# A hybrid block and a second layer on one core: order of weight splits, token splits and norm broadcasts changed in eight places

## The reference, cut to what matters

```
h = concat(meta[16], x[512])                       # 528 tokens, 1024 wide
z = rmsnorm(h) @ w_in                              # conv a, b | c_q 256 | c_kv 128 | k_rope 32
conv = silu(layernorm(conv31(a * sigmoid(b)) + conv_b))            # depthwise, 512 channels, 31 taps
attn = causal attention, 8 heads, 64 + 32 rotated dims, q from c_q, k and v from c_kv
h += concat(rmsnorm(attn), rmsnorm(conv)) @ w_out
h += peer_ffn(rmsnorm(h))                          # 128 of 16384 experts per token, 2 x 64 keys, 8 heads
x = rmsnorm(h)[16:]                                # g_final, 512 tokens
xn = rmsnorm(x)                                    # second layer
q, c_kv, q_idx, k_idx, w_idx, g_attn, x_rnn, g_rnn, merge = split(xn @ w_in_2)
o = attention over the 128 best latent keys of each query (index scores, 8 heads), 16 heads
y_attn = (o * silu(g_attn)) @ w_attn_proj
y_rnn = (rg_lru(conv4(x_rnn)) * silu(g_rnn)) @ w_rnn_proj
x = x + (g_a * y_attn + g_r * y_rnn) @ w_out_2     # gates g = sigmoid(merge + b)
out = rmsnorm(x)
```

## Time and profile before

| | |
|---|---|
| median of 3 runs | 2230.69 us (2230.11 to 2231.13) |
| the profiled execution | 2230.83 us |
| its span in the profile | 2228.9 us |
| TensorE busy | 2113.6 us, 95% |
| DVE / ACT / POOL busy | 1539.5 / 1008.1 / 1009.5 us |
| granted TensorE clock, mean | 0.978 |

### The profile page before, as it was taken

How to read it: one execution, slowest core, us unless ns; L and a number is a source line. 1 busy time by engine, 2 the same in 40 slices (tenths; PEclk the granted TensorE clock), 3 DMA queues, 4 the chain that set the end, 5 groups by cost and what they waited for, 6 DMA issues and landing times. The chain is left out here.

```text
span 2228.9 us, 31197 instructions
## 1 busy us (share of the span) xinstructions
PE 2113.6 (95%) x11527; PEld 1880.3 (84%) x11527; DVE 1539.5 (69%) x2908; ACT 1008.1 (45%) x1858; POOL 1009.5 (45%) x567
## 2 busy tenths in 40 slices
PE   7998999999999999999999999999989989999998
PEld 7754778999999999999999999999867768876676
DVE  4798556759996657778777778876688854017734
ACT  4244433348888733333333333333446652336622
POOL 2200235654455656565566666563324444430052
PEclk8999899999999999999999999999999999999998
DMA  4100023556677899898898989895212222220021
GB/s 179 61 25 1 20 85 126 169 185 236 240 274 278 315 316 341 307 348 315 323 339 323 331 323 339 289 357 174 99 57 76 85 85 104 95 76 1 1 76 57
DMA packets 141589, 414.07 MB, mean 186 GB/s; under 512 B 13056, under 2 KB 57728, under 8 KB 139648
## 3 DMA queue, kind: packets, MB, share of 16 engines
q1 hardware_dynamic: 104576, 277.86, 35.6%
q0 software_dynamic: 36864, 134.23, 16.2%
HBM read 370.62 MB, written 41.42 MB: 185 GB/s over the span
## 5 line engine op out<-in xcount | busy, mean ns | idle before, releaser
L2333 POOL TENSOR_TENSOR wl<-wraw,wh 128x1024 fp32r<-128x1024 f32 x273 | 670.9, 2461 | 885.5 <-ACT wh L1048 884.7
L466 PE MATMUL bank<-XH,wh 128*128 128x384 f32 (+2 forms) x1760 | 631.4, 359 | 16.2 <-issue 8.9
L467 PE MATMUL bank<-XL,wh 128*128 128x384 f32 (+2 forms) x1760 | 624.1, 355 | 0.0
L468 PE MATMUL bank<-XH,wl 128*128 128x384 f32 (+2 forms) x1760 | 619.7, 352 | 0.0
L1048 ACT CAST wh<-wraw 128x1024 fp32r<-128x1024 f32 x362 | 377.9, 1046 | 217.4 <-PE bank L468 209.9
L466 PEld LDWEIGHTS bank<-XH,wh 128*128 128x128 f32 x1760 | 333.5, 189 | 53.6 <-issue 27.0
L466 PE MATMUL bank<-WTH,wh 128*128 128x384 f32 x1024 | 349.6, 341 | 14.3 <-issue 11.9
L468 PEld LDWEIGHTS bank<-XH,wl 128*128 128x128 f32 x1760 | 335.0, 190 | 25.1
L467 PEld LDWEIGHTS bank<-XL,wh 128*128 128x128 f32 x1760 | 333.7, 190 | 26.6 <-issue 2.2
L467 PE MATMUL bank<-WTL,wh 128*128 128x384 f32 x1024 | 347.2, 339 | 0.0
L468 PE MATMUL bank<-WTH,wl 128*128 128x384 f32 x1024 | 347.2, 339 | 0.0
(11 more groups left out here) (457 smaller groups left out, 3102.5 us busy)
## 6 DMA issues: line engine op xcount, KB each, us to landing
wraw<-in_wstream SPq DMA_DIRECT2D x362, 512.0 KB
g_scratch<-gs SPq DMA_DIRECT2D x12, 2048.0 KB
gr<-g_scratch SPq DMA_DIRECT2D x15, 1536.0 KB
a_scratch<-tmp SPq DMA_DIRECT2D x72, 192.0 KB
tmp<-a_scratch SPq DMA_DIRECT2D x46, 192.0 KB
sq<-a_scratch SPq DMA_DIRECT2D x26, 192.0 KB
h<-in_hT SPq DMA_DIRECT2D x8, 264.0 KB, 6.6
fetched<-in_u_rows,diag POOLq DMA_INDIRECT x128
```

Source lines behind the costliest of these rows:

```text
L466: pe.matmul(o, w1, x1, start=n == 0, stop=False)
L467: pe.matmul(o, w1, x2, start=False, stop=False)
L468: m = pe.matmul(o, w2, x1, start=False, stop=n == len(ks) - 1)
L2333: return pool.tensor_tensor(lo, src, hi.bitcast(F32), ALU.subtract)
```

## The change

**1. First layer (`third_product`).** The product "in" 2 goes into the two wide PSUM buffers and stands directly behind the sums; the broadcast stands inside it, ahead of k-tile 4. The diagonals are made from a copy of the identity in PSUM (`ident_first`). Its factors 512 to 527 go to `rest_in`.

The diff, cut to its core:

```diff
+PE_TAPS = 24
+    ident_psum = wide[1][:, 896:1024]
+    ident_first = wide[0][:, 128:256]
@@ conv_schedule
-            if c < 3:
-                taps += [(c, k) for k in range(31)]
+            taps += [(c, k) for k in range(31 if c < 3 else 0)]
             some(("end", c), 4 if c < 3 else 0)
-        for n in range(1, len(UNITS)):
-            some(("norm", n, 0), 2)
-            some(("norm", n, 1), 1)
+        taps += [(3, k) for k in range(PE_TAPS, 31)]
+        for n in range(len(UNITS)):
+            some(("unit", n), 4 if n % 2 else 3)
@@ tensor
+        def third_product():
+            take("wide0", (rb_ready, "in"), (z_out, ("in", 2, 0)))
+            take("wide1", (rb_ready, "in"), (z_out, ("in", 2, 1)))
+            ...
+            for k in range(KT):
+                if k == 4:
+                    for j, (a, m) in enumerate(token_tiles(T)):
+                        ...
+                        pe.wait_ge(*spread.at("in", j))
+                        mm = pe.matmul(o, ones[0:m, :], diag[0:m, j, 0:m], ...)
+                ...
-        broadcast("in", T, wide[1])
-        product(XH, XL, *halves_of(("in", 2), (z_out, ("in", 2))))
+        third_product()
...
-                pe.matmul(wb[:, a:b], qb[0:96, qt * 128:qt * 128 + 128], kb[0:96, a:b], start=True, stop=False,
+                pe.matmul(wb[:, a:b], qb[:, qt * 128:qt * 128 + 128], kb[:, a:b], start=True, stop=False,
@@ tensor, output projection
+            if m == 2:
                 pe.wait_ge(*turned_out.at(31))
                 ... (sums of "oc")
-            if m == 2:
+            if m == 3:
                 broadcast("oa", 512, wide[1])
-            if m == 4:
+            if m == 5:
                 broadcast("oc", 512, wide[0])
@@ tensor, second layer
-        broadcast("fin", 512, wide[0])
...
+        for m in range(2):
+            product(XH, XL, *full(("q", m), (late_out, ("q", m))))
         for m in range(8):
             product(hgh, hgl, *full(("rnn", m), (rnn_mixed, m)), x_ready=hg_ready if m == 0 else None)
         for what in ("q", "ga", "ma"):
-            for m in range(8):
+            for m in range(2 if what == "q" else 0, 8):
                 product(XH, XL, *full((what, m), (late_out, (what, m))))
+                if (what, m) == ("ga", 7):
+                    broadcast("fin", 512, wide[0])
@@ tensor, end
+        for m in range(5):
+            product(mixed_high, mixed_low, *full(("out2", m), (h_added, ("out2", m))), ...)
+        for x in range(2):
+            for m in range(5, 8):
+                ...
+                passes(bank[:, 0:256], n % NSPLIT, mixed_high, mixed_low, 256 * x, 256 * x + 256, None, range(KT), 0, ...)
+                if (x, m) == (1, 5):
+                    end_sums(0)
+                if (x, m) == (1, 6):
+                    end_broadcast(0)
+        end_sums(1)
+        end_broadcast(1)
@@ scalar, attention
+        def normalize(n):
+            act.wait_ge(*recip.at(n))
+            act.mul(Pb[n % 4][:, 0:cols], Pb[n % 4][:, 0:cols], mx[n % 6][:, 2:3]).then_inc(*normed.tell(n))
@@ scalar, experts
+                elif i > 0:
+                    stream()
                 for x in (...)[i] if n == 0 else (i,):
                     weigh_hi(n, x)
                 ...
-            stream()
+            if i == 7 or n + 1 == N_GROUPS or ORDER[n + 1] >= SPILLED:
+                stream()
@@ vector, output projection, second half
         for m in range(8):
-            if m > 0:
-                scaled_lo(GL[:, m - 1, :], ...)
-            if m > 1:
-                add_square(tmp[0][:, 0:512], sq[m % 2][:, 0:512], "ffn", m - 1)
             ... (h[m] += bank)
+            if m > 0:
+                scaled_lo(GL[:, m - 1, :], ...)
+            if m > 2:
+                add_square(tmp[0][:, 0:512], sq[(m - 1) % 2][:, 0:512], "ffn", m - 2)
@@ vector, mix
+        def mixed_lo(m):
+            dve.wait_ge(*x_hi.at("mix", m))
+            minus_high(mixed_low[:, m, :], mixed[:, m, :], mixed_high[:, m, :]).then_inc(...)
...
+            if m > 0:
+                mixed_lo(m - 1)
@@ gpsimd
-        splits_of("two", False)
-        stream(4)
+        splits_of("two", (2, 5))
+        stream(2)
...
-            stream()
-            if c < 7:
-                stream()
+            stream(2)
             pool.wait_ge(*hg_hi.at(c))
@@ weights' order
-    parts += [mg[15:16], rp]
-    parts += [_tiles(q), _tiles(ga), ...]
+    parts += [mg[15:16], q[0:2], rp, q[2:8], _tiles(ga), ...]
```

More of the change, by code:

```diff
@@ L995, in tensor @@
             product(XH, XL, *full(("ya", m), (mixed_step, ("ya", m))), x_ready=og_ready if m == 0 else None)
-        def mix2_ready(m):
-            return (x_hi, ("mix", m)), (x_lo_pool if m % 3 == 1 else x_lo_dve, ("mix", m))
-        for m in range(8):
-            product(XH, XL, *full(("out2", m), (h_added, ("out2", m))), x_ready=mix2_ready if m == 0 else None)
-        pe.wait_ge(*added.at("end", 6))
-        ones_sums(tmp[0], 512, wide[0], 0, True, ("end", "acc"))
-        pe.wait_ge(*squared.at("end", 7))
@@ L1005, in tensor, with end_sums @@
-        ones_sums(sq[0], 512, wide[0], 0, False, "end", last=True)
-        broadcast("end", 512, wide[1])
+        def end_sums(x):
+            pe.wait_ge(*added.at("end", 4))
+            for i, src in enumerate((tmp[0], tmp[1], tmp[2], sq[0])):
+                if i:
+                    pe.wait_ge(*squared.at("end", (i + 4, x)))
+                for j in range(2 * x, 2 * x + 2):
+                    mm = pe.matmul(wide[0][:, j:j + 1], src[:, j * 128:j * 128 + 128], ones[:, 0:1], start=i == 0 and j % 2 == 0,
+                                   stop=i == 3, skip_group_check=True)
+            mm.then_inc(*sums.tell(("end", x)))
@@ new lines, in end_broadcast @@
+        def end_broadcast(x):
+            for j in range(2 * x, 2 * x + 2):
+                pe.wait_ge(*spread.at("end", j))
+                mm = pe.matmul(end_factor[x][:, (j % 2) * 128:(j % 2) * 128 + 128], ones, diag[:, j, :], start=True, stop=True)
+            mm.then_inc(*bcast.tell(("end", x)))
+        def mix2_ready(m):
+            return (x_hi, ("mix", m)), (x_lo_dve, ("mix", m))
+        for m in range(5):
+            product(mixed_high, mixed_low, *full(("out2", m), (h_added, ("out2", m))),
+                    x_ready=mix2_ready if m == 0 else None)
@@ L1090, in scalar @@
         square_in(7)
+        act.wait_ge(*ld_cst.at("cst"))
+        identity("first", ident_first)
         split_hi(2)
@@ L2267, in vector @@
                                      ALU.add).then_inc(*masked.tell(qt))
+        diagonals("fin", 512, 2, after="ckv", ones_at=ident_psum)
+        dve.wait_ge(*bcast.at("fin"))
+        for k in range(KT):
+            dve.scalar_tensor_tensor(hx[k], hx[k], g("g_fin", k), wide[0][:, 0:512], ALU.mult,
+                                     ALU.mult).then_inc(*h_added.tell(("x2", k)))
         dve.wait_ge(*masked.at(3))
@@ L2370, in gpsimd @@
         stream(2)
-        splits_of("ffn", True, FETCH)
+        splits_of("ffn", range(2, KT), FETCH)
         def route(tt):
```

311 lines of the change are left out of this document (185 added, 126 removed).

## The result

| | before | after |
|---|---|---|
| median | 2230.56 us (4 runs) | 2171.64 us (2168.5 to 2172.44, 4 runs) |
| profiled execution, its span | 2230.83, 2228.9 us | 2172.44, 2170.6 us |
| TensorE busy | 2113.6 us | 2090.5 us |
| mean granted clock | 0.978 | 0.986 |

The ratio of after to before is 0.9733, with a 95% interval of 0.9716 to 0.975. The kernel is 59 us faster, where 72 were forecast. 2171.6 lies inside the range of 2144 to 2184 and outside the likeliest case's own range of 2149 to 2168.

The account below looks back on a forecast made before the run. TensorE was taken as the bound, busy 95% of the span, with waits and the half clock behind them to be saved. The terms sum to 72.2 us, 2230.8 to 2158.6 (median 2158.5), range 2144 to 2184 for 8 in 10.

Parts of the forecast that it names:

- First layer: Products 2 and 3 after the sums: waits for diagonals and eviction and half speed go, gain 8.0 us.
- Head of the attention: Start of attention: TensorE's wait for the third of three rotation instructions goes, gain 2.7 us, at worst 0.
- Attention loop: 112 to 203 us: DVE sheds normalizations, rotation instructions and key copies, gains seven taps; 10 us gained of 13.
- End of the attention: 203 to 245 us: latency chain with normalization moved from DVE to ACT, gain 2 us.
- Output projection: DVE's split waits and half clock behind go, 9.0 us; later broadcasts cost 2.8 and 1.3; net 5 us.
- Experts: TensorE's 27 "issue" waits are POOL's, late through ACT's cast; casting one tile earlier gains 20 us, bounds 12 and 22.
- Index stage: Product qi 2 to index scores: faster diagonals from PSUM identity and moved "fin", gain 10.5 us, bounds 5 and 11.
- q 0 and q 1: Placed ahead of the recurrent projection: wait for hgl and half clock go, new wait 2.8 at q 1; net 6 us.
- Mix and end: Mix between ya and out2 gains 6 us; the end by halves, last product to span's end, net 2 us.
- DVE paces: Rival in the spilled expert groups: DVE needs 8.87 against TensorE's 8.50 per two tiles; 2168.5 us, chance 0.2.
- issue waits stay: Rival in the experts: the waits are TensorE's own, so the change there does nothing; 2178.6 us, chance 0.04.
- ACT takes DVE's place, and the broadcasts eat the gain: Rival in attention and output projection: gains 4 and 0 in place of 12 and 5; 2171.5 us, chance 0.17.

Follow-up runs that it names:

- The rotation alone: Kernel before with one DVE rotation instruction on 64 partitions instead of three on 32 per head, key copies for four heads, scores over 128 rows: 2225.1 us, ratio 0.9961.
- that part alone: Kernel before with only DVE's new order in the output projection's second half (add result, split previous tile, square the one before): 2221.3 us, ratio 0.995.
- the edit alone: Kernel before with only ACT's weight casts moved one step in the expert groups whose next U was spilled: 2206.0 us, ratio 0.9876.
- the control's: The changed kernel itself, unedited, timed again beside three experiments on the same chip: 2171.6 us, ratio 0.9727 to the kernel before.

## Why the prediction was right, and where not

Sign and range held; the sum was 14 us too high. That it came so near is in part luck: the experts' term was 5 us too low, and five others were too high by 2 to 5 us each. By the prediction's own steps:

- **First layer** (8.0): 7.6 in the trace. Right. No experiment took this part alone.
- **Head of the attention** (2.7): the wait fell only from 2.7 to 2.0. The term took it as one for the third of three rotation instructions; but the earlier trace rows names L1681, the second, so only one instruction of 0.7 us left its way. The head as a whole lost 0.4; why it lost more than this is not traced.
- **Attention loop** (10 of the 12): 8.8. The size was nearly right and the reason was not. The rotation alone gives 7.0. The normalization, 7.5 of the 13 us counted as work off DVE, gives nothing: with it back on DVE the loop is as fast (87.9 us in both). Seven taps back on TensorE cost 3.5. TensorE is the next limit, and it came sooner than the count of DVE's instructions said.
- **End of the attention** (2 of the 12): 3.2 lost. This is the step that failed. I took the normalization on ACT as a gain for the chain of latency; undoing it gains 6.3 us there. In the profile of the changed kernel that price is a stretch of 17.1 us at half clock, and with the layer norm moved it is longer waits. I had the queue behind ACT's exponential as the lower bound's mechanism; the clock I had only as the rival that ends slower, and for the wrong place, the loop.
- **Output projection** (5 net): 2.8 net. The gain of 9.0 was right (9.3 with that part alone). The price was 8.2 in place of 4.1: the wait at m=4 came out at 2.72 for 2.8, but the second one was mis-sized, 2.27 for 1.3, and 3.4 us at half clock followed each, which I had given only to the lower bound. Its place was wrong, too: it is the eviction, not the convolution's low parts. The rest of the account is 3.4 us at half clock (from 252.2) that the kernel before had early in this stage and that cost it 1.7: 9.3 + 1.7 - 8.2 = 2.8.
- **Experts** (20): 25.1 in the trace, 26.2 with the edit alone. Mechanism right, size low. DVE kept none of the 21.7 us, and the 3.4 us at half clock behind the wait of 2.3, at 1535.6, went as well, 1.7 more: 23.4. The remaining 2 us have no row.
- **Index stage** (11.4 up to the scores): 11.3. Right in sum; of its two reasons only the moved "fin" can carry it, since the "kx" diagonals' time makes no difference to the scores, and "fin" was not taken alone. The prediction read the earlier trace rows as 1.8 us for each diagonal beside POOL. That is a mean of unequal ones: in the trace one took 0.3 and three took 2.4, each as long as one of POOL's subtractions. So both rules of the Trainium skill that were cited ("SBUF — State Buffer", "SBUF: two separate sides"; "VectorE: DVE Perf Modes", "Why PSUM operands drop a tier") agree with this case: one DVE instruction of 2.4 us beside one subtraction of 2.40 from SBUF, four of 0.34 from PSUM. But the bound of 5 that I hung on them was wrong, since the time does not depend on the diagonals. Instead the next stretch, to 1601.01, lost 2.7 us: DVE is late for ckv's factors, and TensorE waits 1.8 and 1.5 us for it, where it waited 0.7 and 1.4, with 3.4 us at half clock behind.
- **q 0 and q 1** (6): 3.8, from 49.4 us of lead at 1601.01 to 52.3 plus 0.8 for the moved broadcast. There is one wait of 2.14, as forecast in kind (POOL's low part of a weight tile behind hgl), but on the projection's own first tile and not on q 1. 3.4 us at half clock and a new wait of 1.16 at 1834 took the rest.
- **Mix and end** (6 + 2): 6.0 together. The first out2 product follows ya without a wait (2112.99) and without half clock, which is the mix's 6 (not taken alone in any run). The end's halves cost inside the products what they save behind them.

The rivals: "DVE paces" and "issue waits stay" are refuted by the cast alone. "ACT takes DVE's place, and the broadcasts eat the gain" is what happened in its two places, which cost 6.3 and 8.2 us. With it alone the forecast had 2171.5, and 2171.6 was measured; that agreement is luck, since the experts gave more and the projections less than it says.

## What to carry to other kernels

Look for the place of a cast or copy in its engine's own list before anything else. One step earlier was worth 25 us here, and the list of waits called its waits "issue" or gave them to another engine. When load moves off a full engine, ask what the next limit is. Give a new TensorE wait of 1 to 3 us a range, from its own length to about twice that, since half clock may follow and may not. A moved broadcast has to be set against the eviction that waits for it, bank by bank. Before a trace's gain is given to an edit, compare the clock of the two stretches: 4 of the 11 us that the rotation seemed to give lay where its profile merely had no half clock.

## What the runs showed of the hardware

- Equal waits have unequal sequels, between kernels: after a wait of 1.05 us the clock stayed at half for 17.1 us in five profiles, and after 1.07 us it stayed full in three, with the same instructions of TensorE ahead of it.
- They also have unequal sequels in the same kernel: behind the wait of 2.14 us at 1769.8 the clock was at half for 3.4 us in the changed kernel's profile, and behind the same wait (2.17 at 1770.5) it stayed full in the control's; behind the wait of 2.20 at 76.2 it was the other way round.
- The spread of a kernel's own executions goes with the clock: the kernel before took 2229.1 us at a mean clock of 0.978 and 2241.5 at 0.971.
- A diagonal of 128 x 128 made by DVE from SBUF took 0.27 to 0.29 us with POOL idle, and 2.4 us when POOL's subtraction of 2.3 to 2.4 us ran: it ended about 0.1 us behind the subtraction. From PSUM it took 0.34 us beside the same subtraction.
